# First norm of a fused two-block kernel: eleven rooms for the first 16 modulation blocks, and a state space product split between VectorE and GpSimd

## The reference

```python
c_act = silu(c)
mod = (c_act @ ada_w + ada_b)[:, None, :]              # 1024 x 6144 weights, 24 MB
sh1, sc1, gt1, sh2, sc2, gt2 = split(mod, 6)
h = rms_norm(x, norm_mix_g) * (1.0 + sc1) + sh1        # 512 tokens x 1024
p = h @ w_in                                            # all four mixers and their gates

# the state space mixer (s5): the parameters alone give its kernels
mag = exp(lam_re * dt); ab = mag * (cos(lam_im * dt), sin(lam_im * dt))
bb_re = q_re * b_re - q_im * b_im
bb_im = q_re * b_im + q_im * b_re
# x[t] = ab * x[t-1] + bb @ u[t];  y = c_re x_re - c_im x_im + d u
```

## Time and profile before

| | us |
|---|---|
| median of three runs | 2319.56 |
| lowest, highest | 2309.91, 2321.72 |
| span of the profiled execution, first to last instruction | 2315.7 |
| PE busy in it | 2147.8 (93%) |
| DVE busy | 1296.3 (56%) |
| POOL busy | 846.9 (37%) |
| chain that ended last | PE 74%, DVE 14%, DMA 7% |

### The profile page before, as it was taken

The page is one execution under the profiler, slowest core; times in us unless marked ns, Lnnn a source line. Parts: engine busy times, 40 slices in busy tenths (PEclk is TensorE's granted clock), DMA queues, the critical chain, the costliest instruction groups (busy, mean ns, idle before and its releaser), DMA issues.

```text
span 2315.7 us, 27377 instructions
## 1 busy us (share of the span) xinstructions
PE 2147.8 (93%) x10790; PEld 1703.9 (74%) x10790; DVE 1296.3 (56%) x1824; ACT 456.1 (20%) x839; POOL 846.9 (37%) x1009
## 2 busy tenths in 40 slices
PE   6889798998799999989989999999899989999996
PEld 5668586676588888866767878787766668878784
DVE  6775655436763243674444745637636747727274
ACT  2112301210100000313342211113133432102011
POOL 1323233232244444432214444444432224444442
PEclk7999899997799999999999999999999989999998
DMA  8867577576799999985528989898965449899885
GB/s 280 221 141 167 114 151 145 121 181 161 229 236 196 196 192 193 192 174 115 108 57 194 194 184 195 179 200 187 197 136 101 92 102 186 178 198 191 184 193 141
DMA packets 121783, 393.60 MB, mean 170 GB/s; under 512 B 25220, under 2 KB 27396, under 8 KB 121272
## 3 DMA queue, kind: packets, MB, share of 16 engines
q0 software_dynamic: 96624, 350.46, 71.3%
q1 hardware_dynamic: 25032, 41.39, 5.6%
HBM read 387.92 MB, written 3.92 MB: 169 GB/s over the span
## 4 chain that ended last, share of the span: by engine, by line
PE 74%; DVE 14%; DMA 7%; issue 2%; ACT 1%; POOL 1%; SPq 0%; DVEq 0%; ACTq 0%; POOLq 0%
PE ps L1582 62%; DMA w_lo<-in_w 4%; PE ps L1710 2%; DMA arena<-in_ada 2%; PE ps L1611 2%; PE ps L1739 2%; PE ps L1725 1%; DVE work L668 1%; PE ps L1896 1%; DVE g_lo L462 1%; POOL w_lo L429 1%; DVE arena L556 1%; DVE arena L669 1%; DMA w_hi<-in_w 1%; DVE small L855 1%
## 5 line engine op out<-in xcount | busy, mean ns | idle before, releaser
L1582 PE MATMUL ps<-h_hi,w_hi 128*128 128x512 f32 x1760 | 711.1, 404 | 27.1 <-DVE h_lo L512 13.3
L1582 PE MATMUL ps<-h_hi,w_lo 128*128 128x512 f32 x1760 | 690.1, 392 | 0.0
L1582 PE MATMUL ps<-h_lo,w_hi 128*128 128x512 f32 x1760 | 690.0, 392 | 0.0
L424 POOL DMA_DIRECT2D w_hi<-in_w x334 | 187.4, 561 | 1289.9 <-PE ps L1582 1203.3
L1582 PEld LDWEIGHTS ps<-h_hi,w_hi 128*128 128x128 f32 x1760 | 332.6, 189 | 126.2 <-issue 29.9
L1582 PEld LDWEIGHTS ps<-h_hi,w_lo 128*128 128x128 f32 x1760 | 332.8, 189 | 71.3
L1582 PEld LDWEIGHTS ps<-h_lo,w_hi 128*128 128x128 f32 x1760 | 333.4, 189 | 64.8 <-issue 2.2
L429 POOL TENSOR_SCALAR w_lo<-w_hi 128x1024 fp32r<-128x1024 f32 x334 | 359.5, 1076 | 45.3 <-DMA w_hi<-in_w 39.8
L1582 PE MATMUL ps<-g_hi,w_hi 128*128 128x512 f32 (+1 forms) x792 | 313.8, 396 | 28.6 <-DMA w_lo<-in_w 19.5
L432 POOL DMA_DIRECT2D w_lo<-in_w x334 | 301.0, 901 | 106.0 <-POOL w_lo L429 106.0
L1582 PE MATMUL ps<-g_lo,w_hi 128*128 128x512 f32 (+1 forms) x792 | 307.1, 388 | 0.0
(11 more groups left out here) (373 smaller groups left out, 2080.1 us busy)
## 6 DMA issues: line engine op xcount, KB each, us to landing
w_hi<-in_w POOLq DMA_DIRECT2D x334, 512.0 KB, 4.0
w_lo<-in_w POOLq DMA_DIRECT2D x334, 512.0 KB, 5.8
arena<-in_ada SPq DMA_DIRECT2D x40, 512.0 KB, 9.4
x<-in_ada SPq DMA_DIRECT2D x8, 512.0 KB, 7.9
x<-in_xT SPq DMA_DIRECT2D x1, 2048.0 KB, 10.0
x<-in_xT SPq DMA_DIRECT2D x4, 512.0 KB, 4.4
arena<-in_memT SPq DMA_DIRECT2D x2, 1024.0 KB, 7.1
out_y<-arena SPq DMA_DIRECT2D x4, 512.0 KB, 2.6
```

What stands on the lines that cost most here:

```text
L424: pool.dma_start(w_hi[:, q % SLOTS, :], A["w"][q]).then_inc(S(f"high_in{q % SLOTS}"), 16)
L1582: mm = pe.matmul(bank, w[:, slot, cols], a(k), start=(k == 0 and i == 0), stop=(k == blocks - 1 and i == 2))
```

## The change

The first eleven pieces get rooms of their own (three more, two of them in a stretch of the arena that is free so early), and SP issues all eleven at once. Piece 11 waits for VectorE's first read, 12 to 14 for its second to fourth, 15 for its seventh. A semaphore now stands for two pieces (`ada_first0` to `ada_first4` for pieces 0 to 9, `ada_first5` for pieces 10 and 15), so that VectorE waits for both pieces of a pair.

VectorE reads its twelve pieces first, and forms f[0] (three instructions) behind them, then the reciprocal of the norm. GpSimd forms f[1] in three instructions, after a new semaphore `s5_powers`, and it now does this ahead of its first weight loads, which no longer wait for `ada_used`. TensorE does both modulation sums first, then waits for f[1] and for the norm's first block, transposes f (into banks 4 to 7), computes tiles 0 to 2, then makes the s5 products, then tiles 3 to 9. ScalarE copies e and kern after the norm's eight blocks. In SP's stream pieces 16 to 19 now stand ahead of the trip of `kern` through DRAM, and pieces 20 to 23 behind it.

```diff
-ADA_PE, ADA_FIRST = 4, 8
+ADA_PE, ADA_FIRST = 4, 11
 def ada_landed(q):
+    if q < 10:
+        return f"ada_first{q // 2}", 32
     if q < 16:
-        return f"ada_in{q % ADA_FIRST}", 16 * (q // ADA_FIRST + 1)
-    return f"ada_in{q % ADA}", 32 + 16 * ((q - 16) // ADA + 1)
+        return ("ada_first5", 16 * (q // 15 + 1)) if q in (10, 15) else (f"ada_in{q - 11}", 16)
+    return f"ada_in{q % ADA}", 16 * ((q - 16) // ADA + 2)
+def first_room(q):
+    return q if q < ADA_FIRST else q - ADA_FIRST + ADA_PE
...
             for q in range(16):
-                if ADA_FIRST <= q < ADA_FIRST + ADA_PE:
-                    sp.wait_ge(S("ada_taken"), q - ADA_FIRST + 1)
-                elif q >= ADA_FIRST + ADA_PE:
-                    sp.wait_ge(S("ada_used"), q - ADA_FIRST - ADA_PE + 1)
-                sp.dma_start(first_slots[q % ADA_FIRST], A["ada"][q]).then_inc(S(ada_landed(q)[0]), 16)
+                if q >= ADA_FIRST:
+                    sp.wait_ge(S("ada_used"), q - ADA_FIRST + (3 if q == 15 else 1))
+                sp.dma_start(first_slots[first_room(q)], A["ada"][q]).then_inc(S(ada_landed(q)[0]), 16)
...
+            sp.wait_ge(S("h_ready"), KT)
+            sp.dma_start(lora, A["lora"]).then_inc(S("lora_in"), 16)
+            for q in range(16, 16 + ADA):
+                ada_piece(q, ada_second["ada"])
             sp.wait_ge(S("s5_kern"), 2)
...
-            sp.wait_ge(S("h_ready"), KT)
-            sp.dma_start(lora, A["lora"]).then_inc(S("lora_in"), 16)
-            for q in range(16, 24):
+            for q in range(16 + ADA, 24):
                 ada_piece(q, ada_second["ada"])
...
-            pool.wait_ge(S("ada_used"), 2)
+            pool.wait_ge(S("s5_powers"), 1)
+            pool.tensor_tensor(im, by_step(0), by_channel(1), ALU.mult).then_inc(S("pool_step"), 1)
+            pool.tensor_tensor(im_tmp, by_step(1), by_channel(0), ALU.mult).then_inc(S("pool_step"), 1)
+            pool.wait_ge(S("pool_step"), 2)
+            pool.tensor_tensor(im, im, im_tmp, ALU.add).then_inc(S("s5_f_imaginary"), 1)
             for q in range(ahead):
                 load_high(q)
...
-            complex_product(f, (by_step(0, 0), by_step(1, 0)), (by_channel(bb[:, 0]), by_channel(bb[:, 1])), blocks4(tmp))
-            do(dve.tensor_scalar(c_in[:, 1], c_in[:, 1], -1.0, None, ALU.mult), "s5_f")
+            do(dve.tensor_scalar(c_in[:, 1], c_in[:, 1], -1.0, None, ALU.mult), "s5_powers")
             modulate(0, ADA_PE, 8)
+            modulate(1, 0, 8)
+            do(dve.tensor_tensor(f[0], by_step(0, 0), by_channel(bb[:, 0]), ALU.mult))
+            do(dve.tensor_tensor(blocks4(tmp), by_step(1, 0), by_channel(bb[:, 1]), ALU.mult))
+            do(dve.tensor_tensor(f[0], f[0], blocks4(tmp), ALU.subtract))
             norm_start()
-            modulate(1, 0, 8)
             modulation(0, 2)
```

More of the change, by code:

```diff
@@ L252, in build @@
         ada_first = {"sum": arena[:, 2048:4096].rearrange("p (a b) -> p a b", a=2)}
-        first_slots = [arena[:, at:at + D] for at in [base_at + D * i for i in range(ADA_FIRST - 2)] + [4096, 4096 + D]]
+        first_slots = [arena[:, at:at + D] for at in [base_at + D * i for i in range(7)] + [18432, 18432 + D, 4096, 4096 + D]]
         ada_second = {"ada": x[:].rearrange("p k t -> p (k t)").rearrange("p (a b) -> p a b", a=ADA),
@@ L429, in load_low @@
                 pool.tensor_scalar(w_lo[:, q % SLOTS, :], w_hi[:, q % SLOTS, :].bitcast(F32), -1.0, 0.0,
-                                   ALU.mult, ALU.add).then_inc(S("negated"), 1)
-                pool.wait_ge(S("negated"), q + 1)
+                                   ALU.mult, ALU.add).then_inc(S("pool_step"), 1)
+                pool.wait_ge(S("pool_step"), q + 3)
                 pool.dma_start(w_lo[:, q % SLOTS, :], A["w"][q], accum_op=ALU.add).then_inc(S(f"low_in{q % SLOTS}"), 16)
-            pool.wait_ge(S("ada_used"), 2)
+            m = s5_m
+            im, im_tmp = (v.rearrange("p s (j c) -> p s j c", j=Q) for v in (m["f"][:, 1], m["e"][:, 0]))
+            by_step = lambda part: m["pw"][:, part, :, 0:Q].unsqueeze(3).broadcast_to((P, S5T, Q, 16))
+            by_channel = lambda part: m["bb"][:, part].unsqueeze(2).broadcast_to((P, S5T, Q, 16))
+            pool.wait_ge(S("s5_powers"), 1)
[3 more added lines that the diff above has]
+            pool.tensor_tensor(im, im, im_tmp, ALU.add).then_inc(S("s5_f_imaginary"), 1)
             for q in range(ahead):
@@ L1308, in _ @@
                                   ps[6 + g][:, 0:P].rearrange("p (s c) -> p s c", c=16), ACT.Copy), "s5_kern")
-            high_shifted(lambda k: mod[:, k:k + 1])
             skip(6)
@@ L1773, in _ @@
             halves = [slice(0, 64), slice(64, 128)]
-            pe.wait_ge(S("s5_f"), 1)
+            modulation(0)
+            modulation(1)
+            pe.wait_ge(S("s5_f_imaginary"), 1)
+            pe.wait_ge(S("norm_scaled"), 1)
             for i in range(4):
                 for s in range(4):
-                    mm = pe.transpose(ps[i][:, P * s:P * s + P], m["f"][:, i // 2, 4 * (i % 2) + s, :], K("ident"))
+                    mm = pe.transpose(ps[4 + i][:, P * s:P * s + P], m["f"][:, i // 2, 4 * (i % 2) + s, :], K("ident"))
                 mm.then_inc(S("s5_turned"), 1)
+            project(3, "dve_freed", ready=h_tile)
+            pe.wait_ge(S("s5_e"), 4)
             for s in range(S5T):
@@ L1784, in _ @@
             mm.then_inc(S("s5_products"), 2)
-            modulation(0)
-            modulation(1)
-            pe.wait_ge(S("s5_e"), 4)
-            project(10, ["dve_freed"] * 6 + ["act_freed"] * 4, ready=h_tile)
+            project(7, ["dve_freed"] * 3 + ["act_freed"] * 4)
             modulation(2)
```

5 lines of the change are left out of this document (3 added, 2 removed).

## The result

The changed kernel is slower: 2321.78 us in the median of 21 runs (2313.48 to 2326.99), against 2316.64 us for the kernel before in as many runs beside them (2309.91 to 2323.87). The ratio is 1.0022, with a 95% interval of 1.0012 to 1.0031: 5.1 us more, where 0.7 less was forecast: the change costs time where a small gain was expected, and the interval leaves no doubt about the sign.

What follows compares the result with a forecast made beforehand. The start was taken as bound by room for pieces, not DMA rate, and VectorE's read of piece 23 as what is handed on. -6.6 + 5.9 = -0.7 us against 2319.56 gave 2318.9, rounded 2319; range 2309 to 2328.

Steps and rivals of the forecast that it cites:

- Until the norm: First part of the sum: VectorE reads group 1 earlier, so the norm begins at 51.7 us, 6.6 us earlier.
- GpSimd does hold VectorE: Group 1 reads: GpSimd's three instructions each hold VectorE for 2.1 us, 6.4 in all, bounds 0 and 9.6.
- the later one waits: SBUF port shared by GpSimd and VectorE: the later instruction blocks fully; cited rows show 1.40 against 0.17 us.
- the transposes cost nothing: TensorE's 16 transposes (3.65 us) behind the norm's first block: costed at nothing, since TensorE catches up with VectorE.
- the products (3.75 us) cover the wait for `w_lo`: s5 products behind tile 2, 4.09 us, cover TensorE's 1.19 us wait for weights before tile 3: net +2.9.
- the landing of pieces 20 to 23: Group 2, behind the trip of `kern`: pieces issued until t + 27.7 land at t + 39.1.
- t + 40.4 (+5.9): Last read of piece 23, counted from tile 1's start: t + 40.4, +5.9 us against 34.5 before.
- trip until the eight reads: SP's write of `kern` to DRAM until its reads may start: 6.8 us, upper end 12.1.
- the estimate of 20 us: SP's 3 MB beside POOL's weights get half of 301 GB/s: 20 us from t + 22.6, +3.6 more.
- slower: the trip holds back pieces 20 to 23: Rival, chance 0.15: in SP's stream, trip 12.1 and landing 10.4 give +7.1 us, 2326.7.
- A later step: TensorE's meeting with VectorE at L1800: TensorE comes about 3.7 us earlier, waits longer, takes nothing from VectorE.
- the forecast of -0.7: Sum for the last read of piece 23: -6.6 + 5.9 = -0.7 us, 105.7 instead of 106.43; chance 0.45.

Runs made afterwards that it cites:

- after_third: The changed kernel a third time, nothing altered: norm at 51.91 us, last read of group 2 at 110.63.
- e9: The changed kernel with the eight reads of `kern` replaced by two of 128 partitions x 4 KB, the same 1 MB: ratio 1.0004 to the kernel before.
- e10: The changed kernel with the eight reads of `kern` replaced by eight of 128 KB in 1 KB rows over 128 partitions: ratio 1.0016 to the kernel before.
- e4: The kernel before with the trip of `kern` put between pieces 16 to 19 and 20 to 23 in SP's stream: ratio 1.0029 to the kernel before.
- after_again: The changed kernel once more, nothing altered: norm at 51.63 us, last read of group 2 at 110.99.
- e2: The kernel before with the eleven rooms alone; f, trip and group 2 as before: ratio 0.9990 to the kernel before.
- e7: The kernel before with the eleven rooms and the whole trip of `kern` behind pieces 20 to 23: ratio 0.9982 to the kernel before.
- e1: The changed kernel with pieces 20 to 23 ahead of the trip of `kern` in SP's stream: ratio 0.9988 to the kernel before.
- e5: The changed kernel with the write of `kern` in place, its wait and eight reads moved behind pieces 20 to 23: ratio 0.9989 to the kernel before.

## Why the prediction was wrong

**Until the norm its times were right.** The first read came at 20.70 (predicted 20.25), the last of group 1 at 42.85 (44.0), the norm at 51.31 (51.7), tile 1 at 64.92 (65.3). GpSimd does hold VectorE: 5.1 us over the three reads, against 6.4 taken and bounds of 0 and 9.6. Its own instructions were longer than assumed, 2.48 to 3.21 us instead of 2.1, and some of that length is waiting. In after_third VectorE was idle for a piece until 22.05 and GpSimd's first instruction took 1.93 us, where it took 2.48 beside a read:

```profile
20.29 1.93 POOL L446 TENSOR_TENSOR arena<-arena 128x1024 f32<-128x1024 f32 x1 [19.84 <-DVE arena L1012]
```

By the lock of SBUF — State Buffer, "Who interferes with whom" (the Trainium skill), whichever comes later blocks until the other is done. The trace agrees that each is held up by the other; it can't show whole-instruction blocking, since 8.6 us of GpSimd held VectorE for 5.1. Nor do rows 5 show that the later one waits, as the prediction said: there VectorE's instruction starts first, at 118.97, and still ends with GpSimd's. Two more steps held: the transposes cost nothing, and the products (3.75 us) cover the wait for `w_lo` ahead of tile 3, which is gone.

**The term that failed is the landing of pieces 20 to 23**, "t + 40.4 (+5.9)", with t for the start of tile 1. Measured it was 111.64 - 64.92, t + 46.7. By its steps:

| step | predicted | measured |
|---|---|---|
| write of `kern` issued | t + 15.7 | 80.37, t + 15.5 |
| trip until the eight reads | 6.8 | 1.75 |
| last of pieces 20 to 23 issued | t + 27.7 | 88.6, t + 23.7 |
| from there to its landing | 11.4 (3.5 + 7.9) | 21.0 |
| its read | 1.3 | 1.96 |

The trip was overpriced by 5 us and the landing underpriced by 9.6. I had priced the 1 MB of the eight reads by its bytes, 3.5 us at 301 GB/s, and added a usual landing of 7.9. Two things were missing. The first: 3 MB in one queue beside the weights take about 20 us even over all 128 partitions. From the first of the replaced reads to the last piece's landing e9 took 102.6 - 83.56 = 19.1 us, e10 104.3 - 84.30 = 20.0. In these stretches 3.15 of 5.81 and of 6.01 MB were SP's, about half. These two bear out the estimate of 20 us that the prediction drew from the Trainium skill (DMA: Bandwidth & Descriptors, "Queues, rings and completion order"): the rule agrees with the traces, and I gave it too little weight. The second: the real reads go onto 16 partitions each, and with them the same stretch took 109.6 - 82.12 = 27.5 us (27.2 and 25.4 in the other two executions). e9 and e10 end at t + 39.2 and t + 39.9 (tile 1 taken at norm + 13.6), next to my t + 40.4. That nearness is luck: the first omission and the overpriced trip cancelled, and what sets the real reads apart from e10's is what is left of the error.

Of the rivals, "slower: the trip holds back pieces 20 to 23" had the right place and sign, and decided, as it said, once piece 23 was read later than t + 41.1. Its price came from the wrong cause: it blamed a trip of 12.1 us, and the trip was 1.75, the landings 21. e4 shows that 12 us do occur where the write stands behind four pieces.

**A later step failed too.** TensorE was to come to its meeting with VectorE 3.7 us earlier than before. It came at 139.8 us against 138.1, 1.7 later; its waits for `w_lo` up to 170 us had risen from 1.9 to 4.9. This decided nothing, as VectorE came later still.

**The base was a late execution.** The sum started from 58.30 and 106.43 us. Against the other two executions of the kernel before (53.2 to 53.6) the gain ahead of the norm is not 6.6 but 1.8 us (51.6 against 53.4 in the mean), and the part behind it costs 59.5 - 47.9 = 11.6 us in the mean (predicted 5.9). So the forecast of -0.7 rests on 6.6 us of gain of which the usual start leaves 1.8. The timed runs of before scatter from 2309.91 to 2323.87 (and one beside after_again and after_third took 2325.48), and both kinds of start may be in them. Their ratio gives a loss of 5.1 us, where the profiles of the last read give 4.7 against the late execution and 10.0 against the mean of the other two (111.1, the mean of three, less 106.4 or 101.1). How often the kernel before starts late wasn't measured, nor what delays its pieces then. With eleven rooms (e2 and e7, norm at 52.85 and 52.73) VectorE did not wait at all, and the changed kernel's norm stayed within 0.6 us in three executions, so a steadier start may be what the rooms give; so few executions don't show it.

From norm to last read the changed kernel thus loses about 6 us by what sets the real reads apart from those of e9 and e10 (59.5 against 53.1), about 3 by the place of pieces 20 to 23 at the end of 3 MB (53.1 against 50.2, the mean of e1 and e5, where VectorE does not wait for them), and about 2 by the rest of the change, to which the products behind tile 2 belong (50.2 against 47.9; 2.9 were predicted for the products). Set against it is a gain of 2 to 7 us ahead of the norm. e1, e5 and e4 show that order alone makes and unmakes the slowdown; how it divides rests on single profiles and is an estimate.

## What to carry to other kernels

When a transfer is moved in front of others in a queue, price it by the rate of a row in which transfers of its own shape ran alone, and by all bytes between it and the last one that someone waits for, not by its own bytes at the mean rate. A second engine that holds up the critical one gives nothing: moving f behind the norm, with the products, was worth about 7 us, moving half of it to GpSimd nothing. Before building a sum on one execution, look at how a start that depends on landings repeats.

## What the runs showed of the hardware that was not expected

- Eight reads of 128 KB onto 16 partitions each landed 3.8 to 14.2 us after issue (median 8.8), and the four 512 KB pieces behind them 14.5 to 21.0. With the same packets over 128 partitions the medians were 6.0 and 10.2.
- A write of 128 KB and the wait for it took 1.75 us where nothing stood ahead in SP's queue (2.9 in e9), 11.7 behind four pieces (e4) and 12.1 on the full queues.
- Eight reads of 128 KB onto 16 partitions each, with next to nothing beside them, moved 151 GB/s at a DMA share of 1.15 (kernel before, 59 to 63 us).
- GpSimd's 128 x 1024 instructions with two inputs took 2.48, 2.90 and 3.21 us beside VectorE's reads, and the first of them 1.93 us with VectorE idle (after_third).
- One and the same kernel ran tiles 1 and 2 at different granted clocks. The changed kernel from 72 to 84 us had 1.00 (2.4 GHz) in two executions and this in after_third, a mean between the levels of 1.2 and 2.4 GHz:

```profile
72.00:84.00 12.00, 12.00 (x91) 10.39 (x90) 6.69 (x7) 0.56 (x2) 3.74 (x5) 0.79 0.87 201
```

The write of `kern` was 1.75 us later there, at 82.12, of which 0.6 us stood already at tile 1 (65.53 against 64.92). The last read of group 2 was no later than in the others, at 110.63. Fewer weights moved beside the reads, 3.95 instead of 4.78 MB from 80 to 112 us, which may be why; no run tests it.
